# The low part of half a tile of h is made on GpSimd instead of VectorE in a hybrid attention and pooling block

## The reference

```python
h = rms_norm(h_res, norm1_g[l]) * (1.0 + sc1) + sh1
proj = h @ w_in[l]
# q (512 columns), k (128), v (128), u (512)
q = apply_partial_rope(rms_norm(q, q_norm_g[l]), cos_q, sin_q)
k = apply_partial_rope(rms_norm(k, k_norm_g[l]), cos_k, sin_k)
attn_out = sliding_window_sink_attention(q, k, v, attn_sinks[l])
pooled = multiscale_pool(u)
pool_out = jnp.einsum('bsgc,gcd->bsgd', pooled, pool_w[l])
pool_out = pool_out.reshape(B, S, POOL_WIDTH) * pool_scale[l]
mixed = jnp.concatenate([attn_out, pool_out], axis=-1) @ w_o[l]
h_res = h_res + g1 * mixed
h2 = rms_norm(h_res, norm2_g[l]) * (1.0 + sc2) + sh2
ff = jnp.square(jax.nn.relu(h2 @ w_mlp_in[l])) @ w_mlp_out[l]
h_res = h_res + g2 * ff
```

## Time and profile before

| what | before |
|---|---|
| median of 3 runs | 980.75 us (980.31 to 983.38) |
| the profiled execution, its own time | 979.74 us |
| its span | 978.0 us |
| TensorE busy | 922.5 us (94%) |
| VectorE busy | 677.9 us (69%) |
| ScalarE busy | 474.7 us (49%) |
| GpSimd busy | 374.4 us (38%) |
| mean granted TensorE clock | 0.996 |

### The profile page before, as it was taken

How to read it: one execution, slowest core, us unless ns; L and a number is a source line. 1 busy time by engine, 2 the same in 40 slices (tenths; PEclk the granted TensorE clock), 3 DMA queues, 4 the chain that set the end, 5 groups by cost and what they waited for, 6 DMA issues and landing times.

```text
span 978.0 us, 12577 instructions
## 1 busy us (share of the span) xinstructions
PE 922.5 (94%) x4381; PEld 763.9 (78%) x4381; DVE 677.9 (69%) x1032; ACT 474.7 (49%) x826; POOL 374.4 (38%) x356
## 2 busy tenths in 40 slices
PE   1898899998999999999999999998999999999998
PEld 1687788776778888788887888886877888888787
DVE  6977888888754587655565545444588656789797
ACT  1745556658464564645544554453344444333341
POOL 8052333335332444988888878830000000000000
PEclk9999999999999999999999999999999999999999
DMA  9851432223322240754465435347998637896673
GB/s 357 323 176 53 129 109 65 74 79 129 108 87 86 87 151 29 240 191 165 162 200 187 160 134 163 139 148 253 344 358 313 217 104 243 292 320 225 213 248 120
DMA packets 92270, 175.53 MB, mean 179 GB/s; under 512 B 9320, under 2 KB 26288, under 8 KB 92208
## 3 DMA queue, kind: packets, MB, share of 16 engines
q1 hardware_dynamic: 92096, 174.70, 53.0%
q10 hardware_dynamic: 112, 0.04, 0.0%
HBM read 136.95 MB, written 37.75 MB: 179 GB/s over the span
## 4 chain that ended last, share of the span: by engine, by line
PE 69%; DVE 12%; ACT 6%; DMA 4%; issue 4%; POOL 3%; SPq 1%; DVEq 0%; ACTq 0%; POOLq 0%
PE psum L1976 22%; PE psum L1978 21%; PE psum L1977 21%; DMA down_raw<-in_w_mlp_out 4%; PE psum L1972 2%; DVE down_operands L1707 2%; ACT probs L778 1%; DVE acc L1153 1%; SPq L618 1%; DVE xh L1227 1%; DVE pT_lo L1269 1%; ACT qT L789 1%; PE psum L2073 1%; ACT hT_hi L724 1%; DVE probs L1294 1%
## 5 line engine op out<-in xcount | busy, mean ns | idle before, releaser
L1976 PE MATMUL psum<-down_operands 128*128 128x512 f32 x448 | 176.0, 393 | 5.9 <-DVE down_operands L1707 5.9
L1063 ACT CAST down_operands<-down_raw 128x1024 fp32r<-128x1024 f32 x96 | 100.9, 1053 | 163.1 <-PE psum L1978 60.4
L1978 PE MATMUL psum<-down_operands 128*128 128x512 f32 x448 | 175.1, 391 | 0.0
L1977 PE MATMUL psum<-down_operands 128*128 128x512 f32 x448 | 174.9, 390 | 0.0
L1707 DVE TENSOR_TENSOR down_operands<-down_raw,down_operands 128x1024 fp32r<-128x1024 f32 x93 | 112.9, 1220 | 29.4 <-ACT down_operands L1063 28.4
L1976 PE MATMUL psum<-h2T,w_operands 128*128 128x512 f32 x272 | 107.5, 395 | 1.8 <-DVE act_quads_a L1653 1.3
L1978 PE MATMUL psum<-h2T,w_operands 128*128 128x512 f32 x272 | 106.0, 390 | 0.0
L1977 PE MATMUL psum<-h2T,w_operands 128*128 128x512 f32 x272 | 105.9, 389 | 0.0
L1976 PEld LDWEIGHTS psum<-down_operands 128*128 128x128 f32 x448 | 84.5, 189 | 26.3 <-DVE down_operands L1707 8.8
L1928 POOL TENSOR_TENSOR w_operands<-raw,w_operands 128x512 fp32r<-128x512 f32 x56 | 83.3, 1488 | 42.1 <-ACT w_operands L1015 42.1
L1978 PEld LDWEIGHTS psum<-down_operands 128*128 128x128 f32 x448 | 84.4, 188 | 17.7
(11 more groups left out here) (247 smaller groups left out, 1931.9 us busy)
## 6 DMA issues: line engine op xcount, KB each, us to landing
down_raw<-in_w_mlp_out SPq DMA_DIRECT2D x160, 256.0 KB, 4.3
down_raw<-act_scratch SPq DMA_DIRECT2D x112, 256.0 KB, 3.3
raw<-in_w_ada SPq DMA_DIRECT2D x32, 512.0 KB, 4.5
raw<-in_w_mlp_in SPq DMA_DIRECT2D x32, 512.0 KB, 4.8
act_scratch<-act_quads_a SPq DMA_DIRECT2D x64, 256.0 KB, 2.1
act_scratch<-act_quads_b SPq DMA_DIRECT2D x48, 256.0 KB, 3.4
slots<-in_w_ada SPq DMA_DIRECT2D x8, 512.0 KB, 10.6
xh<-in_x SPq DMA_DIRECT2D x8, 512.0 KB, 6.0
```

The lines of the kernel that those rows point to most:

```text
L1063: nc.scalar.copy(o[:, 0, :, :], r[:, 0:2, :]).then_inc(op2_hi, 1)
L1976: mm(o, wh, ah, start=first, stop=False, skip_group_check=adds)
L1977: mm(o, wh, al, start=False, stop=False, skip_group_check=adds)
L1978: return mm(o, wl, ah, start=False, stop=last, skip_group_check=adds)
```

## The change

Five of the low halves move from VectorE to GpSimd: in the passes t = 2 to 6 the second half of tile t+1 (tiles 3 to 7). GpSimd makes it between `normalise(t-2, 1)` and the root of q and k of pass t, behind a wait for `h_hi`, that is, for ScalarE's rounding of the same half. It raises a semaphore of its own, and those who waited for `h_lo` now wait for the one or the other.

```diff
+        def h_lo_made(eng, t, h):
+            if t < 3:
+                eng.wait_ge(h_lo, 2 * t + h + 1)
+            elif h == 0:
+                eng.wait_ge(h_lo, 6 + t - 2)
+            else:
+                eng.wait_ge(h_lo_pool, t - 2)
...
                 if t >= 2:
-                    sp.wait_ge(h_lo, 2 * (t - 1))
+                    h_lo_made(sp, t - 2, 0)
+                    h_lo_made(sp, t - 2, 1)
...
                 add_carry(t)
-                if t + 1 < NT:
-                    lo_h(t + 1, 1)
                 add_attn(t - 2, 1)
...
                 if t >= 2:
                     normalise(t - 2, 1)
+                if 2 <= t and t + 1 < NT:
+                    pool.wait_ge(h_hi, 2 * t + 4)
+                    g.tensor_tensor(hTl[:, 4:KD, :], xh[:, (t + 1) % 2, 512:D].rearrange("p (k n) -> p k n", n=P),
+                                    hTh[:, 4:KD, :].bitcast(F32), ALU.subtract).then_inc(h_lo_pool, 1)
                 pool.wait_ge(qk_sums, t + 1)
...
                     if u and k % 4 == 0:
-                        pe.wait_ge(h_lo, 2 * t + k // 4 + 1)
+                        h_lo_made(pe, t, k // 4)
```

More of the change, by code:

```diff
@@ L278, in build @@
         x_turned = sem("x_turned")
-        h_half, h_hi, h_lo = [sem("h_half0"), sem("h_half1")], sem("h_hi"), sem("h_lo")
+        h_half, h_hi, h_lo, h_lo_pool = [sem("h_half0"), sem("h_half1")], sem("h_hi"), sem("h_lo"), sem("h_lo_pool")
         u_done, u_kept = sem("u_done"), sem("u_kept")
```

## The result

| what | before | with the change |
|---|---|---|
| median of 11 runs each | 982.52 us (978.37 to 985.34) | 985.71 us (981.98 to 988.9) |
| ratio, 95% interval | | 1.0039 (1.0025 to 1.0053) |
| span of the profiled execution | 978.0 us | 985.0 us |
| mean granted TensorE clock | 0.996 | 0.996 |

The change costs 0.39%, or 0.0039 x 982 = 3.8 us (2.5 to 5.2 by the interval); the sum of the prediction was 4.2. The page shows nothing of it: TensorE has the same busy time and its 94% as in the earlier trace rows.

The account below looks back on a forecast made before the run. TensorE is busy 94% of the span, so the change costs where TensorE waits, in the mixer: turns of 1.51 + 0.72 + 0.4 + 1.15 + 0.4 = +4.2 us, 980.75 + 4.2 = 985.0, range 982.6 to 987.8.

Parts of the forecast that it names:

- What is removed: Five VectorE instructions of 0.68 us go, 3.4 us in all; attention sums start about 0.2 us earlier in four passes.
- The subtraction: GpSimd's moved 128x512 subtraction takes 1.30 us, first waits for VectorE's low part, and ends at H + 1.67.
- H: The time at which ScalarE's second rounding of h ends in a pass; the moved subtraction can't start before it.
- step 1: Collision at the end of a pass: GpSimd's subtraction holds VectorE's carry's sum, which ends 1.0 us late in pass 4.
- step 2: TensorE's pool_out starts 1.0 us late, a 0.52 us wait absorbs half, and the projection of u is 0.4 us late.
- step 3: The root ends at H + 3.91, so VectorE normalises k 1.51, 1.04, 1.50 and 1.51 us late in passes 2 to 5.
- The turns: Added time from each mixer pass to the next, passes 2 to 7: 1.51, 0.72, 0.4, 1.15 and 0.4 us.
- Rival 1: GpSimd and VectorE don't hold each other up, so pool_out isn't late: +2.2 us, 982.9; chance 0.14.
- Rival 2: The late root is absorbed and only earlier attention sums count: -0.8 us, 979.9; chance 0.06.
- Rival 3: The subtraction costs its highest price, 1.89 us, in each pass: +7.1 us, 987.9; chance 0.10.
- Rival 4: TensorE falls to its low clock once more, costing at most 1.5 us: 985 to 986.5; chance 0.08.
- What follows the mixer: From 225 us on TensorE has its matmuls almost back to back, so nothing takes the mixer's loss back.

Follow-up runs that it names:

- late: The change, but GpSimd makes the root first, then waits for the carry's sum, then makes the moved subtraction: 981.3 us, ratio 0.9999.
- power: Kernel before, plus GpSimd's wait for h_hi and an unused power on 128 x 7 numbers ahead of the root; subtraction stays on VectorE: 986.31 us, ratio 1.0052.
- root_first: The change, but GpSimd makes the root of q and k first and the moved subtraction behind it: 983.05 us, ratio 1.0005.
- passes_2_5: Kernel before, with the change in passes 2 and 5 alone (tiles 3 and 6): 985.73 us, one execution.
- passes_4_6: Kernel before, with the change in passes 4 and 6 alone (tiles 5 and 7): 987.22 us, one execution.
- wait_only: Kernel before, with only GpSimd's wait for h_hi added ahead of the root in passes 2 to 6: 982.74 us, ratio 1.001.
- change_again: The changed kernel once more with no edit, to see what repeats: 988.32 us, one execution.
- late_maxima: The run late, with VectorE making the first maxima of pass 3 ahead of two job pieces in pass 2: 980.59 us, ratio 0.998.

## Why the prediction held, step by step

- **What is removed.** Forecast 0.2 a pass at most, in four passes; `late` shows 0.24 in each of the last three turns. About right, with ScalarE's shift as the next wait, as said.
- **The subtraction.** Forecast 1.30 of its own and 0.29 in which VectorE's low part holds it up, ending at H + 1.67. Measured 1.50 from H + 0.08, ending at H + 1.58; without a collision 1.27, so the hold is 0.23. Right, 0.09 too much.
- **The hold of the carry's sum** (step 1). Forecast 0.08 behind the subtraction's end, some 1.2 us long; measured 0.08 and 1.14. The choice of the row nearer in size (1024 numbers a partition) over that of the power instruction was right, and `power` shows that the other row was right too, for a power on few numbers.
- **TensorE** (step 2). Forecast 0.4 late; measured 0.31, and 0.29 to 0.35 in the turns of `root_first`. The size was 0.1 too high, the 0.09 by which the carry's sum ended earlier.
- **k** (step 3). Forecast H + 3.91; the root ended at H + 3.90 and k started at H + 4.00 to 4.03, since 0.1 lies between the one and the other, which the sum had left out. It is 1.6 late where 1.5 stood, and in pass 3 1.15 where 1.04 stood.
- **The turns.** Forecast 1.51, 0.72, 0.4, 1.15, 0.4; measured 1.37, 0.81, 0.32, 1.15, 0.29. The agreement of the sum (4.2 and 3.93) and of turn 3 to 4 is in part luck. The forecast took k's lateness in pass 3 as 1.04 because in the profile of before k came at H + 2.87 there, and at H + 2.40 or 2.41 in the passes 2, 4 and 5. That late k belongs to one disturbed execution: the attention sums waited 0.27 us for ScalarE's shift, which waited 0.60 for TensorE, from 124 to 126 us, where the granted clock was 0.92 behind 0.73 and 0.50. In pass 3 of `passes_2_5`, with the full clock, k is at H + 2.40. So in an undisturbed kernel before k would be 1.6 later in pass 3 too, and turn 3 to 4 costs 27.48 - 26.30 = 1.2; the prediction's way gives 1.5 - 0.32 = 1.2 for it, and +4.6 in sum, against the 4.5 above. The prediction was right about the one profile and some 0.3 low for an undisturbed kernel; the 3.8 of the timed runs (2.5 to 5.2) tells neither from the other. That in turn 4 to 5 ScalarE's idle times absorb a k that is 1.6 late down to TensorE's delay is borne out by `passes_4_6` (0.37).
- **Rival 1** (no hold) falls by the 1.14, and its +2.2 rested moreover on the root ending earlier. Its mechanism was tried as `power`, with a root even later: a kernel without any hold loses about the same. So the hold, which had the prediction's first step, is the smaller cause: with the root ahead of the subtraction it is worth up to 0.35 a turn, and with the root late it sets turn 6 to w_o (+0.29 against the +0.01 of `power`). A subtraction of full size ahead of the root that nothing holds was not tried.
- **Rival 2** falls in the turns 2 to 3 and 5 to 6, and holds for turn 6 to w_o: `power` loses 0.01 there with k 1.8 late. **Rival 3** falls, with 1497 to 1500 ns in all five. **Rival 4** did not occur in the profile of the change, but in those of `wait_only`, `power`, `passes_4_6`, `change_again` and `late_maxima`; a profile's turn can be 0.2 to 1.4 us longer by it, within the 1.5 that it was given.
- **What follows the mixer.** The prediction says that TensorE has its matmuls almost back to back from 225 us on. In the profile of before it was busy for only 1.73, 0.63 and 1.28 of 2 us in the three stretches from 226 to 232. What was drawn from it, that nothing is given back, held all the same: at 644.8 us of before the change is 4.3 late, the 3.9 of the mixer and the 0.4 ahead of it.

## What to carry to other kernels

Freeing a busy engine pays up to the next wait on it, here 0.24 of 0.68 us; what the work costs on the other engine is set by what stands behind it there. Before work is put on an idle engine, look at what that engine does next and for whom: the same subtraction cost the mixer 3.9 us ahead of the root, 1.0 behind it (4.5 and 1.6 against undisturbed turns), and nothing behind the root and the carry's sum. And compare stages and turns of two profiles rather than their spans, with the granted clock beside each, that of before too: a forecast takes over whatever its one profile happened to have.

## What was not expected of the hardware

- A GpSimd instruction of 512 numbers a partition holds VectorE's sum of two SBUF operands until 0.08 us behind its own end; one on 7 or 10 numbers does not, though it takes longer (1.71 and 1.95 us against 1.27). The Trainium skill (SBUF — State Buffer, Who interferes with whom) has the later instruction block for the whole of the other; the trace agrees for 512 numbers and not for the power instructions. The kernels differ in the operation as well as in the size, and no run parts the two. But the trace of before has a smaller size in it. VectorE's L1303, the smaller of two SBUF operands of 4 numbers, takes 0.27 or 0.28 us in each of the five places where it starts inside GpSimd's L1870, a sum on 96 numbers, and ends 0.02 behind it; elsewhere it takes 0.16, also inside GpSimd's power on one number. First GpSimd, then VectorE, one place of each kind:

  ```profile
  135.06 0.56 POOL L1828 TENSOR_TENSOR small<-small 128x1 f32<-128x1 f32 x1
  155.26 0.39 POOL L1870 TENSOR_TENSOR qkn<-squares 128x96 f32<-128x96 f32 x1
  ```

  ```profile
  135.22 0.16 DVE L1303 TENSOR_TENSOR small<-small 128x4 f32<-128x4 f32 x1
  155.40 0.27 DVE L1303 TENSOR_TENSOR small<-small 128x4 f32<-128x4 f32 x1
  ```

  So additions and subtractions hold from 96 numbers on, in the sizes seen, and powers on 1, 7 and 10 don't.
- One kernel, in the same place and behind the same wait of TensorE, was granted the full clock in one execution and the 1.2 GHz level in another (1.00 against 0.61 and 0.53 from 150 to 154 us, in `change_again`). It cost some 0.2 us in each of two turns there, and up to 1.4 in others. Six of the ten profiles have a low stretch between 90 and 226 us, and each came behind a wait of TensorE, but as these two show, not every such wait brings one: in `root_first` TensorE shows no matmul at all from 120 to 122 us and was granted 1.00 behind it.
